# Two areas of expert weights given back ahead of the router's end, and the table of columns loaded first

## The reference, cut to what matters

```python
logits = jnp.einsum('bsd,de->bse', h, w_router)
scores = jnp.transpose(jax.nn.softmax(logits, axis=-1), (0, 2, 1))
gate, idx = lax.top_k(scores, cap)            # 64 tokens for each of 16 experts
xin = h[bidx, idx]
eo = jnp.einsum('becf,efd->becd', jax.nn.silu(xin @ w_gate) * (xin @ w_up), w_down)
out = out.at[bidx, idx].add(gate[..., None] * eo)
```

## Time and profile before

| what | us |
|---|---|
| median of three runs | 1475.09 (1473.03 to 1475.29) |
| the profiled execution, its own time | 1474.67 |
| its span, from first to last instruction | 1472.9 |
| PE busy | 1375.2 (93%) |
| DVE busy | 546.5 (37%) |
| ACT busy | 339.3 (23%) |
| mean DMA rate | 317 GB/s |

### The profile page before, as it was taken

The page is one execution under the profiler, slowest core; times in us unless marked ns, Lnnn a source line. Parts: engine busy times, 40 slices in busy tenths (PEclk is TensorE's granted clock), DMA queues, the critical chain, the costliest instruction groups (busy, mean ns, idle before and its releaser), DMA issues.

```text
span 1472.9 us, 16602 instructions
## 1 busy us (share of the span) xinstructions
PE 1375.2 (93%) x6689; PEld 743.8 (51%) x6689; DVE 546.5 (37%) x964; ACT 339.3 (23%) x548; POOL 115.3 (8%) x190
## 2 busy tenths in 40 slices
PE   7999899999998898988988989989899999999997
PEld 6778433343333332332323323324378777888876
DVE  6676612121121121111211211113268588756663
ACT  5893110010000010010000100103042365533332
POOL 0000000000000000000000000001022314550000
PEclk9999999999999999999999999999999999999999
DMA  9048899999999999999999999999976123354231
GB/s 322 22 161 337 332 426 405 428 427 426 428 429 429 429 428 428 429 430 428 429 428 429 430 429 428 427 428 429 405 244 156 58 88 90 92 163 141 89 112 57
DMA packets 67827, 467.31 MB, mean 317 GB/s; under 512 B 5760, under 2 KB 30592, under 8 KB 42688
## 3 DMA queue, kind: packets, MB, share of 16 engines
q1 hardware_dynamic: 62864, 454.71, 75.1%
q0 software_dynamic: 4624, 11.44, 3.0%
q10 hardware_dynamic: 288, 0.45, 0.1%
HBM read 458.49 MB, written 7.05 MB: 316 GB/s over the span
## 4 chain that ended last, share of the span: by engine, by line
PE 60%; DMA 32%; DVE 4%; ACT 2%; issue 2%; DVEq 0%; POOL 0%; ACTq 0%
PE bank L961 13%; DMA wide<-in_w_up 11%; PE bank L1019 10%; PE bank L720 8%; PE bank L722 8%; DMA wide<-in_w_down 8%; PE bank L721 8%; DMA early<-in_w_up 8%; DMA early<-in_w_down 6%; PE bank L907 3%; PE bank L1057 2%; PE bank L989 1%; DVE nrm L1724 1%; PE bank L1105 1%; PE bank L1133 1%
## 5 line engine op out<-in xcount | busy, mean ns | idle before, releaser
L961 PE MATMUL bank<-wide,xinT 128*64 128x512 f32 x1376 | 307.2, 596 | 41.8 <-DMA wide<-in_w_up 23.1
L961 PEld LDWEIGHTS bank<-wide,xinT 128*64 128x64 f32 x1376 | 96.3, 137 | 247.9 <-issue 170.7
L961 PE MATMUL bank<-early,xinT 128*64 128x512 f32 x656 | 148.9, 601 | 21.7 <-DMA early<-in_w_up 11.3
L1724 DVE SCALAR_TENSOR_TENSOR th<-th,bank 128x512 f32<-128x512 f32 x32 | 20.6, 684 | 389.3 <-ACT th L1429 389.3
L1019 PE MATMUL bank<-wide,actT 128*64 128x512 f32 x656 | 145.1, 595 | 3.8 <-issue 3.4
L720 PE MATMUL bank<-hT_lo,ring_r 128*128 128x512 f32 x352 | 138.6, 394 | 1.4 <-ACT gt L1297 1.1
L722 PE MATMUL bank<-hT_hi,ring_r 128*128 128x512 f32 x352 | 137.1, 389 | 0.0
L721 PE MATMUL bank<-hT_hi,ring_r 128*128 128x512 f32 x352 | 137.0, 389 | 0.0
L1429 ACT ACTIVATE th<-bank 128x512 f32<-128x512 f32 x32 | 17.4, 595 | 478.6 <-PE bank L961 478.6
L1721 DVE TENSOR_TENSOR ring_r<-ring,ring_r 128x2048 fp32r<-128x2048 f32 (+1 forms) x40 | 89.5, 2236 | 58.3 <-ACT ring_r L1265 57.8
L961 PEld LDWEIGHTS bank<-early,xinT 128*64 128x64 f32 x656 | 46.2, 138 | 122.4 <-issue 80.8
(11 more groups left out here) (423 smaller groups left out, 1660.0 us busy)
## 6 DMA issues: line engine op xcount, KB each, us to landing
wide<-in_w_gate SPq DMA_DIRECT2D x43, 2048.0 KB, 39.0
wide<-in_w_up SPq DMA_DIRECT2D x42, 2048.0 KB, 38.6
wide<-in_w_down SPq DMA_DIRECT2D x39, 2048.0 KB, 38.4
early<-in_w_up SPq DMA_DIRECT2D x21, 2048.0 KB, 38.7
early<-in_w_down SPq DMA_DIRECT2D x21, 2048.0 KB, 38.5
early<-in_w_gate SPq DMA_DIRECT2D x20, 2048.0 KB, 40.2
ring<-in_w_in SPq DMA_DIRECT2D x25, 1024.0 KB, 5.3
ring<-in_w_out SPq DMA_DIRECT2D x8, 1024.0 KB, 4.9
```

Of the source, the lines that this page charges most:

```text
L961: last = pe.matmul(bank[1 + 2 * (m % 2) + q // 2][o:o + 64, :], xinT[:, k, :], w[:, i, q * 512:(q + 1) * 512], start=(k == 0), stop=(k == ...
L1724: return dve.scalar_tensor_tensor(out_, a, s, b, op0, op1)
```

## The change

Areas are placed anew. `ring12` (unit 11 of `w_out`) and `early1` now lie where `lrux`, `conv` and `gt` were; `hi_out` lies over the upper half of `hT`; `xT` lies over `lrux` and `conv`; `score`, `rank`, `top`, `earlier`, `gfb`, `kpos`, `kneg` and the gates' biases go elsewhere. Hence on SP: `w_out` unit 11 waits for the last low part of the recurrence's output instead of `gt_free`, and all that stands behind it on SP waits too; unit 8 of expert 0 is issued right behind it; unit 9 is issued after the logits' product; nothing waits for `sel_ready`. `earlier` is loaded by ACT's queue after the last sum of squares, not by POOL's after the recurrence. `cols` is loaded by ACT right behind `cst`; DVE prepares the two small tables after all four tiles are normalised, and ACT waits for `cols` after its copy of unit 0. `gated(0)` moves behind the running sum, since `score` now lies over `gsel`.

```diff
-        hbias = area("hbias", ends["stat"], 4 * CT + 3 * KT)
-        kpos = area("kpos", ends["hbias"], 2 * CT)
-        kneg = area("kneg", ends["kpos"], 2 * CT)
+        hbias = area("hbias", ends["stat"], 3 * KT)
...
-        ring.append(area("ring12", ends["conv"], UNIT))
-        ring_r.append(area_r("ring12_r", ends["conv"], UNIT))
-        hi_b1 = [ring_r[9], ring_r[5], ring_r[11], area_r("hi_out", ends["conv"] + UNIT, UNIT)]
-        squares = area("squares", ends["lrux"], D)
-        earlier = area("earlier", ends["squares"], S + (TT - 1) * P)
+        xT = [area("xT_a", ends["mixT"], KT // 2, S), area("xT_b", ends["mixT"] + KT // 2 * S, KT // 2, S)]
+        ring.append(area("ring12", ends["xT_b"], UNIT))
+        ring_r.append(area_r("ring12_r", ends["xT_b"], UNIT))
+        last_early = area("early1", ends["ring12"], WIDE)
+        squares = area("squares", ends["early1"], D)
+        earlier = area("earlier", ends["early1"], S + (TT - 1) * P)
+        top = area("top", ends["earlier"], 8, parts=NE)
+        gfb = area("gfb", ends["early1"], D)
+        hi_b1 = [ring_r[9], ring_r[5], ring_r[11], area_r("hi_out", ends["nrm"] + CT * S, UNIT)]
...
-        late = [area(f"early{i}", ends["eo"] + i * WIDE, WIDE) for i in range(EARLY - 1)]
-        early += late[::-1]
-        score = area("score", ends[f"early{EARLY - 2}"], S, parts=NE)
-        rank = area("rank", ends["score"], S, parts=NE)
+        early += [last_early, area("early0", ends["eo"], WIDE)]
+        score = area("score", ends["sel"], S, parts=NE)
+        rank = area("rank", ends["gsel"], S, parts=NE)
...
             sp.wait_ge(gt_free, CT)
+            high_stands(sp, f"lru{CT - 1}")
+            both_stand(sp, f"lru{CT - 1}")
             load(11, w_out_m[:, 2:4, :], D)
+            load_first(8)
             sp.wait_ge(unit_used, 9)
             load_first(2)
             sp.wait_ge(unit_used, 10)
...
             load_first(7)
             sp.wait_ge(*jobs.end("logitT"))
-            load_first(8)
+            load_first(9)
             sp.wait_ge(*jobs.end("logits"))
             load_expert(0, LENT, lent, lent_full)
-            sp.wait_ge(sel_ready, 1)
-            load_first(9)
             load_halves(0, E_UNITS - 1, moe_ring[0], moe_full[0], 0)
...
             act_e.dma_start(cst, cst_d).then_inc(cst_in, 16)
+            act_e.dma_start(cols, cols_d).then_inc(cols_in, 16)
...
-                    if t == 0:
-                        act_e.dma_start(cols, cols_d).then_inc(cols_in, 16)
...
                 elif unit == 11:
-                    act_e.wait_ge(gt_free, CT)
+                    act_e.wait_ge(unit_used, 8)
...
             deviations()
-            act_e.wait_ge(cols_in, 16)
             loaded(act_e, 0)
             act_e.activation(hi_of(0)[:, 0:UNIT // 2], ring[0][:, 0:UNIT // 2], ACT.Copy).then_inc(w_hi, 1)
+            act_e.wait_ge(cols_in, 16)
...
+            act_e.wait_ge(square_sum, 2 * TT)
+            act_e.dma_start(earlier, earlier_d).then_inc(earlier_in, 16)
             copy_out("logitT", logT, bank[jobs.bank("logitT")][:, 0:P])
...
-            pool.wait_ge(lru_done, CT)
-            pool.dma_start(earlier, earlier_d).then_inc(earlier_in, 16)
             roots(8, TT)
...
             for t in range(TT):
-                if t == TT - 1:
-                    dve.wait_ge(cols_in, 16)
-                    link(dve.tensor_scalar(kneg, col("lam", 0, 2 * CT), -1.0, None, ALU.mult))
-                    tt(kneg, kneg, col("lam", 0, 2 * CT), ALU.max).then_inc(halves, 1)
                 dve.wait_ge(deviation, t + 1)
                 link(dve.reciprocal(stat[:, 4 + t:5 + t], stat[:, 4 + t:5 + t]))
                 dve.tensor_scalar(nrm[:, t, :], xres[:, t, :], stat[:, 4 + t:5 + t], None, ALU.mult).then_inc(normed, 1)
+            dve.wait_ge(cols_in, 16)
+            link(dve.tensor_scalar(kneg, col("lam", 0, 2 * CT), -1.0, None, ALU.mult))
+            tt(kneg, kneg, col("lam", 0, 2 * CT), ALU.max).then_inc(halves, 1)
...
             dve.wait_ge(sel_ready, 1)
-            gated(0).then_inc(gsel_ready, 1)
             was_read(dve, "scoreT")
             top_scores(range(2))
...
             tt(rank, rank, score, ALU.mult).then_inc(pos_ready, 1)
+            dve.wait_ge(pos_ready, 1)
+            gated(0).then_inc(gsel_ready, 1)
```

More of the change, by code:

```diff
@@ L176, in build @@
         stat = area("stat", ends["cst"], 64)
-        hbias = area("hbias", ends["stat"], 4 * CT + 3 * KT)
-        kpos = area("kpos", ends["hbias"], 2 * CT)
-        kneg = area("kneg", ends["kpos"], 2 * CT)
+        hbias = area("hbias", ends["stat"], 3 * KT)
         eps = stat[:, 63:64]
-        slot_row = area("slot_row", ends["kneg"], 1, dtype=mybir.dt.uint32)
+        slot_row = area("slot_row", ends["hbias"], 1, dtype=mybir.dt.uint32)
         Z = ends["slot_row"]
@@ L193, in build @@
         gt = area("gt", ends["conv"], 2, 4, S)
-        ring.append(area("ring12", ends["conv"], UNIT))
-        ring_r.append(area_r("ring12_r", ends["conv"], UNIT))
-        hi_b1 = [ring_r[9], ring_r[5], ring_r[11], area_r("hi_out", ends["conv"] + UNIT, UNIT)]
-        squares = area("squares", ends["lrux"], D)
-        earlier = area("earlier", ends["squares"], S + (TT - 1) * P)
-        assert ends["earlier"] <= ends["conv"]
+        xT = [area("xT_a", ends["mixT"], KT // 2, S), area("xT_b", ends["mixT"] + KT // 2 * S, KT // 2, S)]
[7 more added lines that the diff above has]
+        hi_b1 = [ring_r[9], ring_r[5], ring_r[11], area_r("hi_out", ends["nrm"] + CT * S, UNIT)]
         mix_hi = [hT_hi[:, g, :] for g in range(CT)] + [area_r(f"mix_hi{g}", 3 * UNIT + g * S, S) for g in range(CT)]
@@ L205, in build @@
         swapped = area("swapped", max(ends["fold"], ends["sin_part"]), S)
+        gate_bias = area("gate_bias", ends["swapped"], 4 * CT)
+        kpos = area("kpos", ends["gate_bias"], 2 * CT)
+        kneg = area("kneg", ends["kpos"], 2 * CT)
         four_hi = area_r("four_hi", 0, 2, 2, CT, P)
@@ L235, in build @@
         early = [area(f"early{EARLY - 1}", ends["nrm"], WIDE)]
-        late = [area(f"early{i}", ends["eo"] + i * WIDE, WIDE) for i in range(EARLY - 1)]
-        early += late[::-1]
-        score = area("score", ends[f"early{EARLY - 2}"], S, parts=NE)
-        rank = area("rank", ends["score"], S, parts=NE)
-        top = area("top", ends["rank"], 8, parts=NE)
-        xT = [area("xT_a", ends["mixT"], KT // 2, S), area("xT_b", ends["gt"], KT // 2, S)]
+        early += [last_early, area("early0", ends["eo"], WIDE)]
+        assert ends["early0"] <= ends["ring12"]
+        score = area("score", ends["sel"], S, parts=NE)
+        rank = area("rank", ends["gsel"], S, parts=NE)
         qT = area("qT", 0 * UNIT, CT, S)
@@ L279, in build @@
         gsT = area("gsT", ends["tmp"], KT, S)
-        gfb = area("gfb", ends[f"early{EARLY - 2}"], D)
         prep = area("prep", ends["wext"], 24, GP)
@@ L1297, in gates @@
                         read(name, act_e.activation(tile[:, j, :], bank[jobs.bank(name)][:, :], ACT.Tanh, scale=0.5,
-                                                    bias=hbias[:, (2 * d + j) * CT + c:(2 * d + j) * CT + c + 1]))
+                                                    bias=gate_bias[:, (2 * d + j) * CT + c:(2 * d + j) * CT + c + 1]))
                     was_read(act_e, f"lru{c}_{2 * d}")
@@ L1516, in _ @@
                             full(act_e, f"ssm{CT - 1}")
-                        read(name, act_e.activation(dst, src, ACT.Tanh, scale=0.5, bias=hbias[:, 24 + j:25 + j]))
+                        read(name, act_e.activation(dst, src, ACT.Tanh, scale=0.5, bias=hbias[:, KT + j:KT + 1 + j]))
                 if i % 2 == 1 and i < HEADS:
@@ L1551, in _ @@
                 read(name, act_e.activation(ysT[:, n, :], bank[jobs.bank(name)][:, :], ACT.Tanh, scale=0.25,
-                                            bias=hbias[:, 16 + CT + n:17 + CT + n]))
+                                            bias=hbias[:, CT + n:CT + 1 + n]))
             weights_hi(M + 23)
@@ L1766, in _ @@
             weights_lo(1)
-            dve.tensor_scalar(hbias[:, 0:4 * CT], col("bias_lru", 0, 4 * CT), 0.5, None, ALU.mult)
-            dve.tensor_scalar(hbias[:, 4 * CT:4 * CT + 3 * KT], col("b_glu", 0, 3 * KT), 0.5, None, ALU.mult)
+            dve.tensor_scalar(gate_bias, col("bias_lru", 0, 4 * CT), 0.5, None, ALU.mult)
+            dve.tensor_scalar(hbias, col("b_glu", 0, 3 * KT), 0.5, None, ALU.mult)
             wr = col("w_router", 0, KT * 2 * NE).rearrange("p (k e) -> p k e", k=KT)
```

## The result

| | median us | lowest to highest, runs | profiled execution, its span |
|---|---|---|---|
| before | 1474.35 | 1473.03 to 1476.25, 7 | 1474.67, 1472.9 |
| after | 1480.05 | 1479.08 to 1481.0, 7 | 1481.0, 1479.2 |

The ratio is 1.004, with a 95% interval of 1.0031 to 1.005: the change makes the kernel 5.7 us slower. The forecast was 1479.3, inside 1473.3 to 1482.5, and slower was given 0.54.

The account below looks back on a forecast made before the run. PE's path up to the DMA pause at 226 us was taken to set the end. Terms -0.85 + 0.2 + 0 + 4.6 + 0.7 + 0 = +4.65 us on 1474.67 gave 1479.3, range 1473.3 to 1482.5.

Parts of the forecast that it names:

- the gap: DMA engines' last pause, at 226 us before expert 1: PE's gains or losses before it reach the end one for one.
- R2 (rival B): Expert stage: the weight stream is the limit and areas given back early pay; 1465.5 us, chance 0.13 with its milder form.
- `cols` first: Start of the kernel: PE's idle time ahead of its last eight transposes goes; -0.85 us, bounds 0 and -1.0.
- Unit 11: `w_out`'s unit 11, loaded after the last low part, lands in 4.9 us and slightly delays PE; +0.2 us, bounds 0 and 1.7.
- rival C: `w_out`: unit 11 takes 6.4 us to landing and costs 1.7; 1480.8 us, chance 0.60 together with the main case.
- The loads behind it: SP's queue from 129 to 173 us: expert 0's units go later or back to back, none late for PE; cost 0.
- a wider gap at 226: Sign expected in the trace after: the DMA engines' last pause before expert 1 grows; no size given.
- `earlier` late: Before the gather: table issued at 154.07 takes 9.5 us to landing, so DVE counts late; +4.6 us, bounds 1.3 and 6.2.
- R3, rival A: Before the gather: `earlier` lands 5 to 6.5 us after issue, in time or nearly; 1475.1 us, chance 0.27.
- The clock: First gather: more PE idle time makes it start at the lower clock; +0.7 us, bounds -1.9 and 1.5.
- `gated(0)`: DVE, behind the running sum: its 0.7 us lie in DVE's wait until 188 us; cost 0.
- the stream from there on as before: Sign expected after the last DMA pause: the weight transfers run on unchanged; no size given.

Follow-up runs that it names:

- cols_alone: Kernel before, with only `cols` loaded right behind the constants and the two small tables prepared after all four tiles; 1473.03 us, ratio 0.9993.
- cols_busy5: cols_alone (old areas) with five idle products in place of two ahead of the first gather; 1471.64 us, ratio 0.9988.
- tie_late_alone: Kernel before, with only the load of `earlier` moved to ACT's queue after the last sum of squares; 1477.06 us, ratio 1.0022.
- loads_held: Changed kernel, with SP issuing units 6, 7, 9 and 5 of expert 0 only once `earlier` has landed; 1474.77 us, ratio 1.0004.
- areas_late: tie_early with units 8, 9 and 4 of expert 0 issued late (after the logits' product or the selection); 1474.92 us, ratio 1.0009.
- tie_early: Changed kernel, with `earlier` in unit 4's place, loaded by POOL at about 66 us, and unit 4 issued after the selection; 1472.35 us, ratio 0.9989.
- held_less2: Changed kernel, with unit 7 of expert 0 (and 9 and 5 behind it) held until `earlier` is in; 1474.87 us, ratio 1.0007.
- after_filled2: Changed kernel, with 15 idle products in place of 2 on PE ahead of the first gather; 1477.88 us, ratio 1.0026.

## Why the prediction was right, step by step

The reading that carried it was that of the gap: PE's path up to it is what counts. From the start of expert 1 to that of the last unit there pass 845.7 to 846.0 us in the four kernels with the old areas (before, cols_alone, cols_busy5, tie_late_alone) and 844.4 to 845.0 in the six with the new areas and an open gap. So a shift of expert 1 against before appears again at the end, less at most 0.4 us with the old areas and less 1.1 to 1.6 us with the new. In the two whose gap closed, loads_held and areas_late, it is 847.1 and 847.4. R2 (rival B) was right only about these.

1. *`cols` first*: forecast -0.85, measured -1.4. The step was bounded by PE's transposes, "5.36 us from 7.66", taken as fixed. They took 4.23. Nearly every transpose has one of two durations, 421 ns at first (one starts every 0.22 us) and 272 ns later (one every 0.14), and the change between the two comes near 10.3 us in this profile; before, all 24 ran at the slower pace. In cols_alone and tie_late_alone it comes near 12 and in loads_held near 12.7, with a granted clock of 1.00 throughout; why it comes when it does stays open. The releaser of the last eight is still DVE's normalisation, with 0.27 us of idle time before it. The bound of 1.0 was too tight, since a pace was held to be fixed.

2. *Unit 11*: forecast 0.2, measured 0.4; the 4.9 us to landing were exact, and rival C (6.4) did not come.

3. *The loads behind it*: forecast 0, and nothing of expert 0 was late. The pause was to begin at 173 us; it lasts from 172 to 180. The sign "a wider gap at 226" did not come: the room gained went into this pause, and the last gap kept its 1.5 us.

4. *`earlier` late*: forecast 4.6 from 9.5 us to landing, measured 6.9 from 11.8. It is the mis-sized term, and beyond its bound of 11.1. The step took the queue to be "as full at 154 us as at 207", and read `gfb` (11.1) as the far end; in fact a load in work and a whole load queued were ahead of the table. By the list of step 3 unit 7 was to be in by 163, and it came in at 164.2, with the table 0.8 us behind it. Of the 2.3 us, 1.4 are this later landing (165.0 against 163.6). The other 0.9 are PE's own gain: without the wait the counting would have started at 158.1 and not at 159.0, and the table was no earlier for it. The runs put the sizes in order: 3.5 and 4.0 us with empty queues (tie_early, loads_held), 6.1 and 6.3 with one load in work (held_less2, tie_late_alone), 11.8 with one more queued ahead (after, after_filled2). R3, rival A, wanted 5 to 6.5 us in every case; it got that only where no load was queued ahead. The Trainium skill, "DMA: Bandwidth & Descriptors", section "Queues, rings and completion order", has each engine turn from one queue to another after a packet; by that alone a second load queued on SP would make little difference to a table on ACT's queue, and held_less2 against the changed kernel shows 5.7 us between them, which by tie_late_alone the loads behind the table do not explain. The same section says that the signal of completion is an ordered write, which lands only after all earlier writes of that DMA engine, across its queues. The trace agrees with that in so far as the table is told landed 0.8 us after unit 7 and not before it; whether its data were there sooner, no run here shows, since a landing is all that the trace has.

5. *The clock*: forecast 0.7, measured 1.1 (6.49 against 5.37 in the chain). after_filled2 shows that the whole difference to 3.67 is the clock's: the same gather, just as late, at 1.00. The price does not simply follow the idle time ahead of it: 5.37 us after 2.1 us, 4.99 after 3.3 (held_less2) and 6.49 after 9.0.

6. *`gated(0)`*: forecast 0. It runs at 188.68 in 0.69 us, and DVE's next instruction of that helper starts at 195.49 after a wait of 6.12; covered.

The sum of PE's path was forecast as 4.65, against 7.11 at expert 1. Three things brought the end closer to the forecast than its largest term was, and all three are luck. The gain at the start was 0.55 us larger. The stream gave 1.1 us back: "the stream from there on as before" was wrong in that. And the forecast was made from a profiled execution of 1474.67, while the profiled executions differ from the medians by up to 1 us (1481.0 against 1480.05 after). So the mechanism was right and the total is within 0.8 us, but it holds a term that was 2.3 us too small. The lower end of the sum, +0.5, also left out the -1.9 that step 5 had as its own bound; with it that end would be near -1.5.

*What stays open.* The 1.1 us of the stream. Part of it is spread evenly: from the start of one transfer in the chain, at 421 us before, to that of the matching one five experts later, at 715, there pass 293.5 to 293.6 us in the four kernels with the old areas and 293.2 to 293.3 in all eight with the new ones, the two with a closed gap among them. So it goes with the areas and not with the time at which the loads of expert 0 are issued. The order of the loads is the same in both there; the place of `early1` isn't. Why a place should matter was not tried. The 0.6 to 0.7 us of the two pairs of medians fit this, but the gain could also lie elsewhere.

## What to carry to other kernels

Before giving back memory early, look for the last pause of the DMA engines: if one is left behind the point where the loads move, they move into idle time and bring next to nothing. What pays for the room is the danger: a small table that has been displaced from an early load to a late one stands behind 2 MB loads, and its landing must be reckoned from everything that is queued ahead of it, not from the load in work. If it has to be late, hold back the big load that would be queued ahead of it, and look again whether the pause is still there.

## What the runs showed of the hardware

- A table of 448 KB takes 3.5 to 4.0 us with empty queues, 6.1 to 6.3 beside one load of 2 MB in work, and 11.8 with one more queued ahead of it, though that one is on another engine's queue. In all four kernels that issued it from ACT's queue beside loads, it landed 0.8 to 2.1 us after the last load that SP had issued ahead of it; loads issued 1.6 us or more behind it did not hold it up (tie_late_alone). On POOL's queue it took 8.6, right behind two such loads: it landed at 136.4, just after the first (136.2), and did not wait for the second (141.2). What makes the two queues differ, no run here shows.
- The gather of 16 products takes 3.67 us at the granted clock of 1.00, 5.37 and 6.49 us with the clock at 0.50 for a part or nearly all of it. Three more idle products on PE ahead of it took the dip away (1.7 us at no cost), and 13 more did so even through a wait of 7 us.
- At the start the same 24 transposes took 5.36, 4.98 and 4.23 us in three profiles at a granted clock of 1.00, and the first 16 products took 4.1 us in eleven profiles and 5.39 in one, in which the granted clock fell to 0.50. A gain under that size at the start is to be read from medians of many runs, and not from one profile.
